# Two heads' attention scores issued as a pair over 64 contraction rows each, in a two-layer mixer and sparse-attention kernel

## What is computed

```python
s = einsum('bnqhgd,bnkhd->bnhgqk', q_blocks, k_blocks) * 64 ** -0.5
s = where(0 <= distance <= 127, s, -1e30)
m = maximum(max(s), sink); p = exp(s - m); l = sum(p) + exp(sink - m)
o = einsum('bnhgqk,bnkhd->bnqhgd', p / l, v_blocks)
```

## Time and profile before

| | before |
|---|---|
| median of 3 runs | 2204.26 us (2203.4 to 2206.23) |
| the profiled execution | 2206.82 us |
| its span, first to last instruction | 2205.0 us |
| TensorE busy | 2140.5 us (97%) |
| VectorE busy | 1294.4 us (59%) |
| ScalarE busy | 871.9 us (40%) |
| GpSimd busy | 162.4 us (7%) |
| mean granted TensorE clock | 0.993 |

### The profile page before, as it was taken

How to read it: one execution, slowest core, us unless ns; L and a number is a source line. 1 busy time by engine, 2 the same in 40 slices (tenths; PEclk the granted TensorE clock), 3 DMA queues, 4 the chain that set the end, 5 groups by cost and what they waited for, 6 DMA issues and landing times.

```text
span 2205.0 us, 31360 instructions
## 1 busy us (share of the span) xinstructions
PE 2140.5 (97%) x10498; PEld 1748.2 (79%) x10498; DVE 1294.4 (59%) x2291; ACT 871.9 (40%) x1659; POOL 162.4 (7%) x96
## 2 busy tenths in 40 slices
PE   7998999999999999999999999999999999999997
PEld 6577778888888878888888888888888887777775
DVE  7887555666643566466666435555544457556663
ACT  4444453322223266533322332222222355455652
POOL 0042001000001111020000122000000110000001
PEclk9999999999999999999999999999999999999998
DMA  4122102233333311123332333333233334300002
GB/s 161 48 87 59 57 29 86 96 96 99 99 96 105 103 41 38 42 94 105 95 95 95 99 111 96 95 95 96 96 102 97 95 89 133 104 20 20 20 11 76
DMA packets 49472, 180.83 MB, mean 82 GB/s; under 512 B 5488, under 2 KB 5616, under 8 KB 49264
## 3 DMA queue, kind: packets, MB, share of 16 engines
q1 hardware_dynamic: 49248, 179.25, 26.0%
q0 software_dynamic: 144, 0.52, 0.1%
HBM read 177.66 MB, written 2.10 MB: 82 GB/s over the span
## 4 chain that ended last, share of the span: by engine, by line
PE 83%; DVE 4%; ACT 3%; issue 2%; DVEq 0%; POOLq 0%; ACTq 0%; POOL 0%
PE pj L2178 69%; PE po L2540 3%; PE ps L2500 2%; PE po L2395 2%; PE pt L2515 2%; PE ps L2349 2%; PE pt L2365 1%; DVE rtmp L1437 1%; ACT w_both L716 1%; DVE s_sb L1490 1%; PE pj L2318 1%; PE po L2404 0%; PE ps L2489 0%; ACT pT L830 0%; DVE w_both L1300 0%
## 5 line engine op out<-in xcount | busy, mean ns | idle before, releaser
L2178 PE MATMUL pj<-h_hi,w_both 128*128 128x512 f32 x3472 | 1121.8, 396 | 17.1 <-DVE w_both L1300 13.7
L2178 PEld LDWEIGHTS pj<-h_hi,w_both 128*128 128x128 f32 x3472 | 653.9, 188 | 156.8 <-issue 16.1
L2178 PE MATMUL pj<-h_lo,w_both 128*128 128x512 f32 x1736 | 677.4, 390 | 0.0
L716 ACT ACTIVATE w_both<-raw 128x1024 fp32r<-128x1024 f32 x321 | 340.0, 1059 | 820.6 <-PE pj L2178 811.5
L1300 DVE TENSOR_TENSOR w_both<-raw,w_both 128x1024 fp32r<-128x1024 f32 x296 | 400.0, 1351 | 303.5 <-ACT w_both L716 303.2
L2178 PE MATMUL pj<-G_hi,w_both 128*128 128x512 f32 x1408 | 440.4, 392 | 3.4 <-DVE G_lo L1649 2.2
L2178 PEld LDWEIGHTS pj<-h_lo,w_both 128*128 128x128 f32 x1736 | 327.3, 189 | 64.7 <-issue 1.4
L2178 PEld LDWEIGHTS pj<-G_hi,w_both 128*128 128x128 f32 x1408 | 264.9, 188 | 62.0 <-DVE w_both L1300 4.6
L2178 PE MATMUL pj<-G_lo,w_both 128*128 128x512 f32 x704 | 274.6, 390 | 0.0
L2178 PEld LDWEIGHTS pj<-G_lo,w_both 128*128 128x128 f32 x704 | 132.5, 188 | 26.6
L628 POOL TENSOR_TENSOR ssum<-sq 128x512 f32<-128x512 f32 x6 | 9.2, 1533 | 1439.1 <-ACT sq L953 1439.1
(11 more groups left out here) (335 smaller groups left out, 2324.0 us busy)
## 6 DMA issues: line engine op xcount, KB each, us to landing
raw<-in_wstream SPq DMA_DIRECT2D x330, 512.0 KB, 3.5
xT<-in_x SPq DMA_DIRECT2D x4, 512.0 KB, 8.5
out_x<-xT SPq DMA_DIRECT2D x4, 512.0 KB, 2.7
memT<-in_mem SPq DMA_DIRECT2D x1, 1024.0 KB, 12.2
cst<-in_cst SPq DMA_DIRECT2D x1, 512.0 KB, 10.3
tab<-in_tab POOLq DMA_DIRECT2D x1, 512.0 KB, 5.3
posi<-in_pos SPq DMA_DIRECT2D x1, 256.0 KB, 2.8
vec<-in_vec SPq DMA_DIRECT2D x1, 182.5 KB, 2.4
```

The source lines that it names most:

```text
L716: nc.scalar.activation(w_hi[:, c.par * CW:(c.par + 1) * CW], raw[:, c.par * CW:(c.par + 1) * CW], ACT.Copy).then_inc(hi_ready, 1)
L2178: mm = nc.tensor.matmul(acc, w[:, col:col + P], x[part], start=first and k == 0, stop=last and k == 2)
```

## The change

In the three attentions the keys are no longer masked and stored twice: `b_k` has a column block for each key head, with that head's keys both in rows 0 to 63 and in rows 64 to 127, and `mem_k` is one plain copy of the projection. A score takes only the 64 rows of its head, of the queries and of the keys. The units of a tile now alternate between the heads, block by block, so units u and u + 1 (u even) are the two heads of one block. In steps of even u the scores of units u + 2 and u + 3 are issued one right after the other; in odd steps none is issued. The local attention's tiles are written out instead of looped. `aq` keeps its order.

```diff
@@ Attention
-        self.ahead = 3 if self.m == 8 else 2
+        self.ahead = 2
@@ _attentions
-    pair = [(hh, b) for hh in range(2) for b in range(NB)]
+    pair = [(hh, b) for b in range(NB) for hh in range(2)]
@@ attention_tiles
-            if ph.name == "aq":
+            if ph.name in ("aq", "bq"):
                 for j in range(ph.tiles):
                     tile(ph, 0, j)
                 return
@@ GpSimd
             pool.wait_ge(x_ready, RESIDUALS["down0"] + DT)
-            nc.gpsimd.memset(b_k[:, :], 0.0).then_inc(zeroed, 1)
@@ ScalarE, memory keys
-                        act.wait_ge(chunk_used, c.v + 3)
-                        for hh in range(2):
-                            last = nc.scalar.activation(mem_k[l][:, (2 * k + hh) * MEM:(2 * k + hh + 1) * MEM],
-                                                        pj[t.par][:, 0:MEM], ACT.Copy, scale=V("half", hh))
-                        last.then_inc(pj_free[t.par], 1)
+                        take(mem_k[l][:, k * MEM:(k + 1) * MEM], t, c, n=MEM)
@@ VectorE, spread_keys
-                        col = ((2 * pair + g) * 2 + hh) * S
+                        col = (2 * pair + g) * S
@@ VectorE, ahead of rope_keys
-            dve.wait_ge(zeroed, 1)
@@ TensorE, score_
+                rows = slice(0, P) if branch == "topk" else slice(hh * 64, hh * 64 + 64)
                 if branch == "topk":
                     keys = a_k[:, j % 4 * S:j % 4 * S + w]
                 elif branch == "mem":
-                    k_at = (2 * t + hh) * MEM
-                    keys = mem_k[0 if ph.name == "amem" else 1][:, k_at:k_at + MEM]
+                    keys = mem_k[0 if ph.name == "amem" else 1][rows, t * MEM:(t + 1) * MEM]
                 elif branch == "band":
-                    keys = b_k[:, sl(g * 2 * S + hh * S + k0, w)]
+                    keys = b_k[rows, sl(g * S + k0, w)]
 
                 pe.wait_ge(score_taken, ph.first_score + t * ph.n + u + 1)
-                nc.tensor.matmul(ps[u % 2][:, 0:w], q[:, par * S + b * P:par * S + (b + 1) * P], keys,
+                nc.tensor.matmul(ps[u % 2][:, 0:w], q[rows, par * S + b * P:par * S + (b + 1) * P], keys,
                                  start=True, stop=True).then_inc(score_done, 1)
@@ TensorE, tile
                 for u in range(ph.n):
                     p, v = ph.split(u)
-                    score_(ph, i, j, u + ph.ahead)
+                    if ph.m == 4:
+                        score_(ph, i, j, u + ph.ahead)
+                    elif u % 2 == 0:
+                        score_(ph, i, j, u + 2)
+                        score_(ph, i, j, u + 3)
                     turn_p(ph, i, j, u + 1)
                     values(ph, i, j, u)
```

More of the change, by code:

```diff
@@ L1147, in _ @@
             pieces = [(which, part) for which in range(2) for part in range(2)]
-            act.wait_ge(zeroed, 2)
+            act.wait_ge(zeroed, 1)
             def window_hi(k):
@@ L1213, in _ @@
                     act.wait_ge(v_turned, TN["cmpv"] + 1)
-                    act.wait_ge(zeroed, 3)
+                    act.wait_ge(zeroed, 2)
                     for b in range(NB):
@@ L1443, in spread_keys @@
                     for hh in range(2):
-                        col = ((2 * pair + g) * 2 + hh) * S
-                        last = nc.vector.tensor_copy(dst[hh * 64:hh * 64 + 64, col:col + S], ktmp[g * 64:g * 64 + 64, pair * S:(pair + 1) * S])
+                        col = (2 * pair + g) * S
+                        last = nc.vector.tensor_copy(dst[hh * 64:hh * 64 + 64, col:col + S],
+                                                     ktmp[g * 64:g * 64 + 64, pair * S:(pair + 1) * S])
                 return last
```

## The result

The changed kernel takes 2256.5 us (median of 4 runs, 2255.13 to 2258.08), the kernel before 2205.24 us (4 runs beside them, 2203.4 to 2210.09). The ratio is 1.0221, 95% interval 1.0202 to 1.0239: some 50 us slower. The forecast was 2233 us with a range of 2216 to 2243. The direction was right, the size was not, and the time lies outside the range.

The account below looks back on a forecast made before the run. TensorE, busy 97% of the span, was taken as the bound. Local +17.5 and memory +11.6 us, with -4.6 inside them, gave 29.1; on 2206.8 that is 2235.9, set 2.5 lower to 2233 us, range 2216 to 2243.

Parts of the forecast that it names:

- The bound: Whole kernel: TensorE, busy 97% of the span, sets the time, so every wait its queue gains is paid in full.
- The pair's price: Scores of the three attentions: a pair costs 0.73 us wide, 0.52 narrow; 4.6 us saved over 48 pairs.
- The walk of the local tile: Local attention: step-by-step count of TensorE's waits; a tile gains 2.43 us, the stage 17.5 us.
- The rotation's product: Local tile, VectorE: the query rotation's first product, held by GpSimd's split, would last near 2.3 us.
- the pair of step 4: Local tile: this pair waits 1.14 us for unit 5's late maximum to free PSUM; unit 5's turn waits 0.49.
- Rival 1: Local attention: the rotation's first product is not held by GpSimd's split; stage +7.4 us, total 2223 us; chance 0.26.
- the hold: Local tile: GpSimd's split blocks VectorE's first rotation product until T+3.9, T being step 2's pair start; unit 5's maximum 1.6 late.
- The walk of the memory stage: Both memory attentions: the short lead makes TensorE wait 1.06 us a pair; period 3.06 for 2.20, +5.8 us each.
- T+2.30: Memory attentions: the turn of the probabilities can begin 2.30 us after the pair's scores start streaming at T.
- The clock: Memory attentions: the sum took TensorE's clock as full and added no time for a fall.
- rival 3: Memory attentions: the clock falls to half, a pair's period about 3.7 us, 9 us more, total 2242 us; chance 0.07.
- Work at nothing: Loop to straight code, GpSimd's key-buffer clearing and four ScalarE copies removed: zero gain, 1 us at best.

Follow-up runs that it names:

- experiments 2 and 5: Against the kernel before: 2, memory scores over 128 rows in the change's order and short lead, 2223.9 us; 5, only local tiles written out, 2206.2 us.
- experiment 6: Kernel before with memory scores paired over 64 rows in four PSUM banks, issued two and three steps ahead of their turns; 2217.4 us.
- after: The changed kernel with the whole change, against the kernel before; 2256.5 us, ratio 1.0221.
- the late split: Changed kernel with ScalarE's high part, and with it GpSimd's split, moved from step 2 to step 5 of a local tile; 2243.2 us.

## Why the prediction failed, step by step

- **The bound.** Right: the longer stages add up to 51.2 us, the whole difference of the spans.
- **The pair's price.** Right at full clock: the next instruction 0.63 behind, VectorE after 0.91 (0.84 forecast). The 4.6 us saved are too much: with no short lead, a stage with eight pairs was 0.07 us shorter (six of them within the count). The Trainium skill's doubling (TensorEngine Tiling (Array Packing), Theoretical Speedup) holds for the two scores themselves, 0.63 for two and 0.62 for one. That the work around them gets dearer, 0.29 us a unit with single scores, agrees with the drain at a change of mode that the same page of the Trainium skill states under Key Properties; no run shows the drain by itself.
- **The walk of the local tile**, "+17.5": 17.6 measured, a tile 17.18 (17.2 forecast). The rotation's product 2.28 (2.3); waits for the pair of step 4 and its turn 1.51 together (1.14 + 0.49); around the turn and values of unit 6 0.55 (0.70). These waits are 0.27 less than walked and the tile is the same, so its other work was walked 0.27 too cheap: that the tile fits so closely is in part luck. Rival 1 is out: only by moving the split does the hold go.
- **The walk of the memory stage**, "a period of 3.06", "+5.8 for each": the mechanism was right, the term too small. At full clock the period was 3.23: the turn came at T+2.38 for T+2.30, and 0.86 us lie between it and the next pair for 0.76 (values behind a wait and the 0.10 ahead of the pair take 0.58, not 0.49). With it, at full clock, the stages take 24.9 to 25.7 us: +6.5 to +7.8 each, some 14 for both in place of 11.6. The wait before the turn is 0.91 us, as "about 0.9" said.
- **The clock.** This is the step that failed. The sum took full clock in the memory stages, and rival 3 had a chance of 0.07, with "the waits are near 1 us each, with work between" against it. That argument was true and beside the point: with the start filled, those very waits left the clock at 1.00. The fall belongs to the stage's start, where the prediction took the first wait "as before" and it grew to 1.35 and 2.30 us; with products in that wait the kernel took 13 us less. What I had no notion of is how long the clock then stays down: with scores over 64 rows for most of the stage, over 20 us in each of the seven stages that fell and got no products, where with scores over 128 rows it was back within 4 us both times (experiments 2 and 5). The size of rival 3 was wrong too: "no wait left" gave 3.7 and 9 us. The 3.7 is what pairs without waits take at half clock (experiment 6); with the short lead the turn still waits 0.31 us, and the period is 4.27. So the clock costs 32.3 less 25, 7 us each, and with the 1.8 and 2.6 behind the stages some 19 us, where the sum had nothing and rival 3 said 9.
- **Work at nothing.** Right for the loop: written out, 0.6 us less in the stage. The clearing and the copies were not taken out by themselves.

In sum: 17.6 + 14 + 19 = 51 against 29.1. A hint was in rows before the change: the earlier trace rows showed the clock at half over 2.98 busy us of 3, and I took from them the fall, not that the busy time behind it did not end it at once.

What stays open: why scores over 64 rows keep the clock down. Half the rows at work and the change of mode around each score come together in every kernel here; no run parted them. Why the clock falls behind a wait of 1.35 us in one profile and not, with the same program, in the next is open as well, and so is why it now and then falls in the local attention of one run and not in the next.

## What to carry to other kernels

Two heads over 64 rows cost TensorE as much as one head over 64 rows, but about 0.3 us goes to the places where 64 and 128 rows meet, so a pair of 256-wide scores is worth next to nothing here. Whether longer runs in one mode would pay was not tried. Before an edit shortens the lead of a chain through VectorE and ScalarE, walk the chain; here it cost over 30 us at full clock, and the pairs saved 4.6 at best. Where a stage begins with a wait, read the granted clock behind it as well as the busy time, and ask what work is there to bring it back; a few unused full-row products in the wait are a cheap test (two groups of 1.3 us gave back 13 us here). One profile is not enough to say that a stage keeps its clock: the same stage ran both ways within one execution. None of the kernels here is faster than the kernel before, but for the one with written-out tiles, by 0.1%.

## What was not expected of the hardware

- A stage at 1.2 GHz with TensorE busy for 20.00 of 20 us (64-row scores among 128-row turns and values, behind a wait of 1.68 us), while the same program ran at 2.4 GHz in the other layer with 20.21 of 21 us busy.
- The stage with pairs and waits for a quarter of the time stayed at 2.4 GHz for 21 us (15.64 busy) when it began there.
- Three full-row products of 256 columns (2.72 us at half clock, 313.79 to 316.51) brought it back; with scores over 128 rows it came back by itself (within 4 us, in experiments 2 and 5).
- A single 64-row score of 256 columns holds TensorE for 0.62 us, a pair 0.63; over 128 rows one takes 0.43 to 0.49.
- The same program behind the same two waits (1.35 and 0.92 us) fell to half clock in after and stayed at full clock in the late split, 16.71 of 23 us busy.
